# Seven-product matmul groups: weight sums made by accumulating transfers from POOL's queue, products in another order, two raw buffers in place of three

## The chip, the core and the metric

One core of one Trainium2 chip runs the whole program. The metric is the device time in microseconds from one launch to its end. Engines are named PE (TensorE), ACT (ScalarE), DVE (VectorE), POOL (GpSimd) and SP (SyncE, which here only issues transfers).

## What is computed

A sequence of 512 tokens of width 1024 runs through three transformer layers in float32. What matters here are the three feed-forward parts, two with a squared relu and one gated:

```python
def _mlp(x, w_up, w_down):            # layers "mlp0" and "mlp1", hidden width 4096
    h = jax.nn.relu(x @ w_up)
    return (h * h) @ w_down
# the third, "ffn", hidden width 2816: (silu(x @ w_1) * (x @ w_2)) @ w_ffn_out
```

## The kernel before

**Split matmuls.** Every matmul of the projections runs as three fp32r matmuls: each operand is split into a high part (the value rounded to fp32r) and a low part (the rest), and high x high, high x low and low x high are accumulated in PSUM. One matmul of 128x128 by 128x512 is one of the three.

**Chunks.** Weights come in chunks of at most 2048 numbers a partition (1 MB). Chunk `c` uses slot `c % 2` of three pairs of buffers: `RAW` (as loaded), `WH` (high, written by ACT's `split`, L1450) and `WL` (low, written by DVE's `split`, L2115). SP's `load` waits until `lo_ready` says that chunk c-2 is split, and issues the transfer into its raw buffer. ACT's `split` waits for the transfer (`raw_in`) and for `chunk_done` of c-2, so that the `WH` slot is free. DVE's `split` follows half by half and raises `lo_ready`, on which PE waits before it starts the chunk. Both halves are 1024 wide.

**Stages.** mlp0 and mlp1 have four rounds each, ffn three. A round first makes eight feature tiles (up projection, four chunks, each 48 matmuls) and then multiplies them by the matching rows of the down weights. In the first three rounds of an mlp and the first two of ffn, eight in all and called groups 0 to 7 (`SEVEN`), this second step is a 2x2 block product with seven block products instead of eight. The tiles fall into even and odd ones, the tokens and output columns into halves. Each group has four weight blocks, `block(k, n)` with k the parity of the tile and n the half of the columns, 1 MB each. Sums and differences of the activations are made by DVE tile pair by tile pair while the up projection runs (`first_sum`, `other_sums`, in `SQ_T` and `S_T`) and are split by `pair_high` and `pair_low`. Of the seven weight operands three are blocks and four are sums of blocks.

**A group's chunks** are d to d+6, with d = `SEVEN_AT[g]`; d+7 is the next round's first up chunk. A product is 24 matmuls, on two PSUM banks, and DVE's `taken` (L2170 to L2181) adds or copies them into quadrants of `Y` or common parts in `X` (for ffn in other buffers), which frees the banks for the product after the next. `common_sums` puts the parts together in the following round.

**Weight sums before.** SP loads block(0,0) into the raw buffer of d, block(0,1) into that of d+1, and block(1,1) into a third buffer, `THIRD`, in the arena `ar` (L457). DVE forms the four sums with subtractions: `first_weights` (L2157, one instruction of 2048) before the last pair of tiles, and three pairs of 1024 (L2199, L2210, L2222) between the splits of `seven`. It raises `weight_sums` after each, on which ACT waits for its high halves (`high_half`, L1453) and SP before it loads block(1,0) for d+5 and before d+7. DVE's low halves of these chunks are `low_half` (L2123).

**POOL's stream** is in program order: small statistics, bias and mask loads, and in `load_gb` (L3031) two broadcasts of 512 KB into `GB`. In mlp0 and mlp1 `load_gb` stands in wait of `s_("ln0_y")` or `s_("ln2_y")` for T = 4 tiles. DVE's `plus_bias` (L2501) raises these, one tile for each of the four up chunks of the first round, the fourth within the last chunk, after `first_weights` and `sum_of_even`. So the fourth comes just ahead of groups 0 and 3.

Of the kernel before, what the change touches and what calls it, by code (L numbers as in the profile page):

```python
# [18 lines left out]
P = 128  # L19
# [52 lines left out]
UNLOADED = {d + x for d in SEVEN_AT for x in (2, 3, 4, 6)}  # L72


def raw_loads(c):

    return sum(x not in UNLOADED for x in range(c % 2, c + 1, 2))

# [61 lines left out]
def build(nc, a, out):  # L140
# [11 lines left out]
    def sem(name):  # L152
        return ctx.enter_context(nc.semaphore(name))
# [58 lines left out]
    raw_more = [sem(f"raw_more{s}") for s in range(2)]  # L212
    hi_ready, lo_ready = sem("hi_ready"), sem("lo_ready")
# [35 lines left out]
    weight_sums, third_in = sem("weight_sums"), sem("third_in")  # L249
# [16 lines left out]
    def slot(c):  # L266
        return c % 2

# [121 lines left out]
    S_T, THIRD = cut(0, 768), cut(8192, CH)  # L390
# [35 lines left out]
    def _(sp):  # L426
# [23 lines left out]
        def load_seven(g, down, k0):  # L450

            d = SEVEN_AT[g]
            def block(k, n):
                return down.rearrange("(k two p) n -> p k two n", p=P, two=2)[:, k0 // 2:k0 // 2 + 4, k, 512 * n:512 * n + 512]
            load(d, slot(d), (grid(RAW[slot(d)], 4, 512), block(0, 0)))
            load(d + 1, slot(d + 1), (grid(RAW[slot(d + 1)], 4, 512), block(0, 1)))
            sp.dma_start(grid(THIRD, 4, 512), block(1, 1)).then_inc(third_in, 16)  # L457
            sp.wait_ge(weight_sums, 7 * g + 5)
            load(d + 5, slot(d + 5), (grid(RAW[slot(d + 5)], 4, 512), block(1, 0)))
            sp.wait_ge(weight_sums, 7 * g + 7)  # L460
# [127 lines left out]
    def _(pe):  # L588
# [359 lines left out]
        def seven(g, name, i):  # L948

            d, (_, ra, _, n0, _, _) = SEVEN_AT[g], BASE[name]  # L950
            lower, upper, centre = A[0:2], A[2:4], C
            low, high = [slice(256 * m, 256 * m + 256) for m in range(2)]
            even, odd = [lambda v, p, m, k=k: v[:, 2 * p + k, m] for k in range(2)]
            part = lambda x: lambda v, p, m: v[:, p, 256 * x:256 * x + 256]
            last = i == (1 if name == "ffn" else 2)
            for q, (of, m, event, banks) in enumerate((
                    (even, low, 1, lower), (even, high, 1, upper), (part(1), None, 3, centre), (part(2), None, 3, upper),
                    (part(0), None, 3, centre), (odd, low, 2, upper), (odd, high, 2, centre))):
                pe.wait_ge(lo_ready, d + q + 1)
# [476 lines left out]
    def _(act):  # L1436
        def split(c, per=0, i=0, more=None, halves=(0, 1)):
# [4 lines left out]
            act.wait_ge(raw_in[s], 16 * raw_loads(c) + i * (16 * (per // 2)))  # L1442
# [12 lines left out]
        def high_half(c, src, half):  # L1455

            at = slice(1024 * half, 1024 * half + 1024)
            act.wait_ge(chunk_done, c - 1)
            copy(WH[slot(c)][:, at], src[:, at]).then_inc(hi_ready, 1)

# [6 lines left out]
        def seven(g):  # L1467

            d = SEVEN_AT[g]
            first = RAW[slot(d)]  # L1470
            act.wait_ge(weight_sums, 7 * g + 1)
            high_half(d + 1, first, 0)
            pair_high(g, 3, 0)
            high_half(d + 1, first, 1)
            pair_high(g, 3, 1)
            for half in range(2):
                act.wait_ge(weight_sums, 7 * g + 2 + half)
                high_half(d + 2, first, half)
            pair_high(g, 3, 2)
            act.wait_ge(third_in, 16 * g + 16)  # L1480
            for half in range(2):
                high_half(d + 3, THIRD, half)
            for half in range(2):
                act.wait_ge(weight_sums, 7 * g + 4 + half)
                high_half(d + 4, THIRD, half)
            split(d + 5)
            for half in range(2):
                act.wait_ge(weight_sums, 7 * g + 6 + half)
                high_half(d + 6, first, half)
            split(d + 7)  # L1490
# [608 lines left out]
    def _(dve):  # L2099
# [19 lines left out]
        def low_half(c, src, half):  # L2119

            at = slice(1024 * half, 1024 * half + 1024)
            dve.wait_ge(hi_ready, 2 * c + half + 1)
            x = tt(WL[slot(c)][:, at], src[:, at], f32(WH[slot(c)][:, at]), ALU.subtract)  # L2123
            if half:
                x.then_inc(lo_ready, 1)

# [5 lines left out]
        def first_sum(g, p, ready):  # L2132

            dve.wait_ge(*ready)
            tt(SQ_T[:, 0, 256:512], SQ_T[:, 0, 256:512], SQ_T[:, 1, 256:512], ALU.add).then_inc(pair_sums, 1)  # L2135
            dve.wait_ge(pair_sums, pair_event(g, p, 1))

        def other_sums(g, p):
# [3 lines left out]
            tt(S_T[:, 512:768], SQ_T[:, 1, 0:256], S_T[:, 256:512], ALU.subtract).then_inc(pair_sums, 1)  # L2142
# [8 lines left out]

        def first_weights(g):

            d = SEVEN_AT[g]
            dve.wait_ge(raw_in[slot(d + 1)], 16 * raw_loads(d + 1))
            dve.wait_ge(lo_ready, d + 1)
            tt(RAW[slot(d)][:], RAW[slot(d + 1)][:], RAW[slot(d)][:], ALU.subtract).then_inc(weight_sums, 1)  # L2157
# [25 lines left out]
        def seven(g, name, i, biased=None, ready=None):  # L2183

            d = SEVEN_AT[g]
            raw, other, upper, centre = RAW[slot(d)], RAW[slot(d + 1)], A[2:4], C
            halves = [slice(1024 * half, 1024 * half + 1024) for half in range(2)]
# [5 lines left out]
            low_half(d + 1, raw, 0)  # L2193
            pair_low(g, 3, 0)
            low_half(d + 1, raw, 1)
            dve.wait_ge(third_in, 16 * g + 16)
            dve.wait_ge(lo_ready, d + 2)
            for at in halves:
                tt(raw[:, at], THIRD[:, at], raw[:, at], ALU.subtract).then_inc(weight_sums, 1)  # L2199
            low_half(d + 2, raw, 0)  # L2200
            low_half(d + 2, raw, 1)
            other_sums(g, 3)
            pair_low(g, 3, 1)
            pair_low(g, 3, 2)
            taken(g, 1, five, upper, fresh)
            low_half(d + 3, THIRD, 0)
            low_half(d + 3, THIRD, 1)
            dve.wait_ge(lo_ready, d + 4)
            for at in halves:
                tt(THIRD[:, at], THIRD[:, at], other[:, at], ALU.subtract).then_inc(weight_sums, 1)  # L2210
            taken(g, 2, six, centre, fresh)
            low_half(d + 4, THIRD, 0)
            low_half(d + 4, THIRD, 1)
            if biased:
                dve.wait_ge(*biased)
            taken(g, 3, quadrant(0, 1), upper, kept)
            low_half(d + 5, other, 0)
            low_half(d + 5, other, 1)
            dve.wait_ge(raw_in[slot(d + 5)], 16 * raw_loads(d + 5))
            dve.wait_ge(lo_ready, d + 3)  # L2220
            for at in halves:
                tt(raw[:, at], other[:, at], raw[:, at], ALU.subtract).then_inc(weight_sums, 1)  # L2222
            taken(g, 4, sum_seven(name), centre, fresh)
            low_half(d + 6, raw, 0)
            low_half(d + 6, raw, 1)
            taken(g, 5, quadrant(0, 0), upper, kept)
# [3 lines left out]
        def common_sums(name, g, at):  # L2230
# [6 lines left out]
            for x in range(2):  # L2237
# [3 lines left out]
                elif at == 1:  # L2241
                    dve.wait_ge(common_one, 2 * SUMMED.index(name) + 2)
                    then(tt(quadrant(0, 1)[:, x, :], quadrant(0, 1)[:, x, :], six[:, x, :], ALU.add))
                    tt(quadrant(0, 1)[:, x, :], quadrant(0, 1)[:, x, :], five[:, x, :], ALU.add)
                else:
# [3 lines left out]
                    if name == "ffn":  # L2249
                        z = tt(y, y, five[:, x, :], ALU.add)  # L2250
                    else:
                        then(tt(five[:, x, :], five[:, x, :], seventh[:, x, :], ALU.add))
# [250 lines left out]
        def mlp(name, before, ln, n):  # L2503
# [8 lines left out]
            for i in range(3):  # L2512
                g = (0 if name == "mlp0" else 3) + i
                for j in range(4):
                    split(c0 + 11 * i + j + 1)
                    if j == 3:
                        first_weights(g)
# [416 lines left out]
        for n in range(2):  # L2934
            for p in range(4):
                split(c + 2 * p + 1)
                split(c + 2 * p + 2)
                if p == 3:
                    first_weights(6 + n)
# [47 lines left out]
    def _(pool):  # L2987
# [64 lines left out]
        load_gb(a["ln_mlp_g"][0], a["ln_mlp_b"][0])  # L3052
        pool.wait_ge(s_("toeplitz_out"), 16)
# [16 lines left out]
        load_gb(a["ln_mlp_g"][1], a["ln_mlp_b"][1])  # L3070

# [30 lines left out]
        load_gb(a["norm_gains_2"][0, 3])  # L3102

# [18 lines left out]
```

## Time and profile before

| | |
|---|---|
| time, median of 3 runs | 2385.11 us (2384.94 to 2386.81) |
| profiled execution | span 2384.7 us, no time of its own beside it |
| PE | 2361.6 us, 99% |
| weight loads into PE | 1951.9 us, 82% |
| DVE | 1382.1 us, 58% |
| ACT | 963.6 us, 40% |
| POOL | 73.9 us, 3% |
| transfers | 220.25 MB, 92 GB/s on average |

The span is that of the profiled execution from the first to the last instruction. Busy shares are over the whole span. Matmuls overlap, so two that follow each other every 0.23 us are each shown as 0.39 us long; the distance of their starts is what counts.

### The profile page before, as it was taken

How to read it: one execution, taken by the hardware profiler on the slowest of the kernel's cores; microseconds unless marked ns; L12 is line 12 of the kernel's file. 1: busy time of each engine (PE TensorE's matmuls, PEld its weight loads, DVE VectorE, ACT ScalarE, POOL GpSimd, SP SyncE). 2: the span in 40 equal slices, each digit the busy share in tenths (PEclk: the TensorE clock that was granted, in tenths of full speed). 3: DMA queues.
4: the chain of work that ended last, by engine and by line, in shares of the span. 5: the costliest groups of instructions: out<-in, count | busy, mean ns of one | idle time of the engine just before them, and what ended most of it. 6: DMA issues, size and time to landing. Idle time of an engine off the chain costs nothing.

```text
span 2384.7 us, 29276 instructions
## 1 busy us (share of the span) xinstructions
PE 2361.6 (99%) x11460; PEld 1951.9 (82%) x11460; DVE 1382.1 (58%) x2079; ACT 963.6 (40%) x1731; POOL 73.9 (3%) x148
## 2 busy tenths in 40 slices
PE   8999999999999999999999999999999999999998
PEld 8778888888888888888888888888877888888887
DVE  4667877766678787676545223223356535574655
ACT  4434443325545344345444233332245534433323
POOL 3000000000000000000000001000000000000000
PEclk9999999999999999999999999999999999999999
DMA  4124324332212322323222322223321122323232
GB/s 143 54 73 133 124 79 142 106 106 94 66 54 89 124 89 88 124 89 106 85 75 85 109 89 75 84 71 99 100 71 54 54 88 95 100 71 124 88 123 71
DMA packets 177237, 220.25 MB, mean 92 GB/s; under 512 B 10031, under 2 KB 131084, under 8 KB 176864
## 3 DMA queue, kind: packets, MB, share of 16 engines
q1 hardware_dynamic: 173152, 204.82, 26.8%
q0 software_dynamic: 3968, 13.81, 1.8%
q8 instruction: 81, 1.33, 0.2%
q14 instruction: 36, 0.29, 0.0%
HBM read 216.48 MB, written 5.28 MB: 93 GB/s over the span
## 4 chain that ended last, share of the span: by engine, by line
PE 95%; DVE 3%; ACT 1%; issue 0%; DMA 0%; SPq 0%; DVEq 0%
PE B L590 45%; PE A L590 41%; PE C L590 7%; PE C L1052 1%; DVE ar L2324 0%; DVE WL L2115 0%; PE C L1315 0%; DMA X<-in_x 0%; PE C L1161 0%; DVE Y L2446 0%; DVE st L2427 0%; PE C L657 0%; PE C L876 0%; DVE X L2919 0%; PE A L657 0%
## 5 line engine op out<-in xcount | busy, mean ns | idle before, releaser
L2115 DVE TENSOR_TENSOR WL<-RAW,WH 128x1024 fp32r<-128x1024 f32 (+3 forms) x346 | 395.6, 1184 | 383.4 <-ACT WH L1450 383.0
L590 PE MATMUL B<-XH,WH 128*128 128x512 f32 (+1 forms) x1432 | 542.6, 383 | 1.4 <-ACT XH L1507 0.8
L590 PE MATMUL B<-XH,WL 128*128 128x512 f32 (+1 forms) x1432 | 534.9, 377 | 0.0
L590 PE MATMUL B<-XL,WH 128*128 128x512 f32 (+1 forms) x1432 | 520.4, 379 | 2.9 <-DVE XL L2271 2.8
L1450 ACT ACTIVATE WH<-RAW 128x1024 fp32r<-128x1024 f32 (+4 forms) x362 | 353.0, 1025 | 406.7 <-PE A L590 266.2
L590 PEld LDWEIGHTS B<-XH,WH 128*128 128x128 f32 x1432 | 269.2, 188 | 68.4 <-issue 14.1
L590 PEld LDWEIGHTS B<-XH,WL 128*128 128x128 f32 x1432 | 269.2, 188 | 50.4
L590 PEld LDWEIGHTS B<-XL,WH 128*128 128x128 f32 x1432 | 260.4, 189 | 52.4 <-DVE XL L2271 4.6
L590 PE MATMUL A<-WH,XH 128*128 128x512 f32 (+2 forms) x688 | 260.7, 379 | 0.0
L590 PE MATMUL A<-WH,XL 128*128 128x512 f32 (+2 forms) x688 | 259.2, 377 | 0.0
L590 PE MATMUL A<-WL,XH 128*128 128x512 f32 (+2 forms) x688 | 259.1, 377 | 0.0
L590 PE MATMUL A<-WH,YH 128*128 128x512 f32 x608 | 237.6, 391 | 0.2 <-DVE WL L2115 0.2
L590 PE MATMUL A<-WH,YL 128*128 128x512 f32 x608 | 236.8, 390 | 0.0
L590 PE MATMUL A<-WL,YH 128*128 128x512 f32 x608 | 236.7, 389 | 0.0
L590 PEld LDWEIGHTS A<-WH,XH 128*128 128x128 f32 x688 | 129.5, 188 | 23.8 <-issue 1.0
L590 PEld LDWEIGHTS A<-WH,XL 128*128 128x128 f32 x688 | 129.4, 188 | 23.2
L590 PEld LDWEIGHTS A<-WL,XH 128*128 128x128 f32 x688 | 129.6, 188 | 22.9
L590 PEld LDWEIGHTS A<-WH,YH 128*128 128x128 f32 x608 | 114.1, 188 | 24.9 <-DVE WL L2115 0.7
L590 PEld LDWEIGHTS A<-WH,YL 128*128 128x128 f32 x608 | 114.1, 188 | 24.0
L590 PEld LDWEIGHTS A<-WL,YH 128*128 128x128 f32 x608 | 114.2, 188 | 23.0
L590 PE MATMUL A<-ar 64*128 64x256 f32 (+7 forms) x512 | 112.6, 438 | 0.0
L1453 ACT ACTIVATE YH<-ar 128x512 fp32r<-128x512 f32 (+1 forms) x86 | 51.6, 627 | 133.8 <-DVE ar L2135 81.4
(368 smaller groups left out, 2967.9 us busy)
## 6 DMA issues: line engine op xcount, KB each, us to landing
RAW<-in_w_in SPq DMA_DIRECT2D x33, 1024.0 KB, 5.1
RAW<-in_mlp_w_up SPq DMA_DIRECT2D x32, 1024.0 KB, 5.3
RAW<-in_mlp_w_down SPq DMA_DIRECT2D x26, 1024.0 KB, 5.1
RAW<-in_w_in SPq DMA_DIRECT2D x48, 512.0 KB, 4.5
RAW<-in_w_ffn_in SPq DMA_DIRECT2D x22, 1024.0 KB, 5.1
RAW<-in_w_ffn_out SPq DMA_DIRECT2D x8, 1024.0 KB, 5.0
ar<-in_mlp_w_down SPq DMA_DIRECT2D x6, 1024.0 KB, 7.6
RAW<-in_mla_w_o SPq DMA_DIRECT2D x4, 1024.0 KB, 5.0
```

The source lines that it names most:

```text
L590: return nc.tensor.matmul(dst, l, r, start=first, stop=last)
L1052: r = nc.tensor.transpose(C[kb][:, tok(x)], W_S[:, z, h, blk * P:blk * P + P], ident[:])
L1450: nc.scalar.activation(WH[s][:, part], RAW[s][:, part], ACT.Copy).then_inc(hi_ready, 1)
L1453: return nc.scalar.activation(dst, src, ACT.Copy, scale=scale)
L2115: x = tt(WL[s][:, part], RAW[s][:, part], f32(WH[s][:, part]), ALU.subtract)
```

## The change

- SP loads only three blocks of a group as chunks: block(0,0) into d, block(1,0) into d+1, block(1,1) into d+3 (`SEVEN_PLAIN`).
- POOL issues four transfers that add a block from HBM onto what the raw buffer holds (`add_seven`, `SEVEN_ADDED`): block(0,1) for d+2, block(1,1) for d+4, block(0,1) for d+5, block(1,0) for d+6. Each waits for `lo_ready` of chunk c-2 and raises `raw_added` of its slot.
- `first_weights` and the three pairs of DVE subtractions are gone, with `THIRD`, `high_half`, `low_half`, `weight_sums` and `third_in`. ACT and DVE use the ordinary `split` for all seven chunks.
- The order of the products, their activation operands, the places that `taken` writes and signs in the activation sums and in `common_sums` change to fit.
- In POOL's stream the transfers of groups 0 to 2 stand behind the `load_gb` that waits for `ln0_y`, those of groups 3 to 5 behind that for `ln2_y`, those of 6 and 7 at the end.

```diff
+SEVEN_PLAIN, SEVEN_ADDED = {0: (0, 0), 1: (1, 0), 3: (1, 1)}, {2: (0, 1), 4: (1, 1), 5: (0, 1), 6: (1, 0)}
+ADDED_AT = {d + q for d in SEVEN_AT for q in SEVEN_ADDED}
...
         def load_seven(g, down, k0):
...
-            load(d, slot(d), (grid(RAW[slot(d)], 4, 512), block(0, 0)))
-            load(d + 1, slot(d + 1), (grid(RAW[slot(d + 1)], 4, 512), block(0, 1)))
-            sp.dma_start(grid(THIRD, 4, 512), block(1, 1)).then_inc(third_in, 16)
-            sp.wait_ge(weight_sums, 7 * g + 5)
-            load(d + 5, slot(d + 5), (grid(RAW[slot(d + 5)], 4, 512), block(1, 0)))
-            sp.wait_ge(weight_sums, 7 * g + 7)
+            for q, (k, n) in SEVEN_PLAIN.items():
+                c = SEVEN_AT[g] + q
+                load(c, slot(c), (grid(RAW[slot(c)], 4, 512), seven_block(down, k0, k, n)))
...
             for q, (of, m, event, banks) in enumerate((
-                    (even, low, 1, lower), (even, high, 1, upper), (part(1), None, 3, centre), (part(2), None, 3, upper),
-                    (part(0), None, 3, centre), (odd, low, 2, upper), (odd, high, 2, centre))):
+                    (even, low, 1, lower), (odd, low, 2, upper), (even, high, 1, centre), (part(2), None, 3, upper),
+                    (part(1), None, 3, centre), (part(0), None, 3, upper), (odd, high, 2, centre))):
...
-            act.wait_ge(raw_in[s], 16 * raw_loads(c) + i * (16 * (per // 2)))
+            act.wait_ge((raw_added if c in ADDED_AT else raw_in)[s], 16 * raw_loads(c) + i * (16 * (per // 2)))
...
-            tt(SQ_T[:, 0, 256:512], SQ_T[:, 0, 256:512], SQ_T[:, 1, 256:512], ALU.add).then_inc(pair_sums, 1)
+            tt(SQ_T[:, 0, 256:512], SQ_T[:, 0, 256:512], SQ_T[:, 1, 256:512], ALU.subtract).then_inc(pair_sums, 1)
...
             first_sum(g, 3, ready)
-            low_half(d + 1, raw, 0)
+            split(d + 1, halves=(0,))
             pair_low(g, 3, 0)
-            low_half(d + 1, raw, 1)
-            dve.wait_ge(third_in, 16 * g + 16)
-            dve.wait_ge(lo_ready, d + 2)
-            for at in halves:
-                tt(raw[:, at], THIRD[:, at], raw[:, at], ALU.subtract).then_inc(weight_sums, 1)
-            low_half(d + 2, raw, 0)
-            low_half(d + 2, raw, 1)
+            split(d + 1, halves=(1,))
             other_sums(g, 3)
             pair_low(g, 3, 1)
+            split(d + 2)
             pair_low(g, 3, 2)
...
+            taken(g, 1, quadrant(0, 0), upper, kept)
+            split(d + 3)
+            taken(g, 2, five, centre, fresh)
+            split(d + 4)
             taken(g, 3, quadrant(0, 1), upper, kept)
...
+            split(d + 5)
+            taken(g, 4, six, centre, fresh)
+            split(d + 6)
+            taken(g, 5, sum_seven(name), upper, fresh)
             split(d + 7)
             taken(g, 6, quadrant(1, 0), centre, kept)
...
                     split(c0 + 11 * i + j + 1)
-                    if j == 3:
-                        first_weights(g)
                     sum_of_even(squared(i, j, 0))
...
         pool.wait_ge(s_("ln0_y"), T)
         load_gb(a["ln_mlp_g"][0], a["ln_mlp_b"][0])
+        def add_seven(g, down, k0):
+            for q, (k, n) in SEVEN_ADDED.items():
+                c = SEVEN_AT[g] + q
+                pool.wait_ge(lo_ready, c - 1)
+                pool.dma_start(grid(RAW[slot(c)], 4, 512), seven_block(down, k0, k, n), accum_op=ALU.add).then_inc(raw_added[slot(c)], 16)
+        for i in range(3):
+            add_seven(i, a["mlp_w_down"][0], 8 * i)
         pool.wait_ge(s_("toeplitz_out"), 16)
```

## Rows read from the trace of the kernel before

**Rows 1.** The page, part 1: busy us, share, instructions of each engine.

```profile
PE 2361.6 (99%) x11460; PEld 1951.9 (82%) x11460; DVE 1382.1 (58%) x2079; ACT 963.6 (40%) x1731; POOL 73.9 (3%) x148
```

**Rows 2.** Waits of PE: releaser, us in total, times, longest.

```profile
PE B L590 <- DVE WL L2115: 0.3, 1, 0.3
```

**Rows 3.** Chain in order of time, 772 to 812: start us, us, what.

```profile
772.73 10.89 PE A L590 x48
...
794.61 5.62 PE C L590 x24
...
805.69 5.75 PE C L590 x24
```

**Rows 4.** The same chain, 2241 to 2281.

```profile
2241.92 10.88 PE A L590 x48
...
2258.29 5.49 PE A L590 x24
...
2274.72 5.44 PE C L590 x24
```

**Rows 5.** Timeline of PE, ACT, POOL and SP: start us, us, engine, line, operation.

```profile
772.57 0.39 PE L590 MATMUL A<-WH,YH 128*128 128x512 f32 x1
...
796.42 2.01 ACT L1450 ACTIVATE WH<-RAW 128x1024 fp32r<-128x1024 f32 x2 [4.39 <-DMA RAW<-in_mlp_w_down]
...
773.83 0.56 POOL L3031 DMA_DIRECT2D GB<-in_ln_mlp_g  x1 [143.94 <-DVE Y L2501]
774.38 0.55 POOL L3031 DMA_DIRECT2D GB<-in_ln_mlp_b  x1
...
242.31 0.37 SPq L438 DMA_DIRECT2D RAW<-in_mlp_w_down  x1
242.72 0.84 SPq L457 DMA_DIRECT2D ar<-in_mlp_w_down  x1
```

**Rows 6.** DVE groups by form: busy us, mean ns, idle before.

```profile
L2199 DVE TENSOR_TENSOR RAW<-ar,RAW 128x1024 f32<-128x1024 f32 x16 | 18.9, 1222 | 0.8
...
L2157 DVE TENSOR_TENSOR RAW<-RAW 128x2048 f32<-128x2048 f32 x8 | 18.3, 2292 | 0.8
```

**Rows 7.** Timeline of DVE around group 3.

```profile
766.59 2.35 DVE L2115 TENSOR_TENSOR WL<-RAW,WH 128x1024 fp32r<-128x1024 f32 x2
...
772.31 1.22 DVE L2501 TENSOR_TENSOR Y<-Y,GB 128x1024 f32<-128x1024 f32 x1
...
776.37 1.22 DVE L2123 TENSOR_TENSOR WL<-RAW,WH 128x1024 fp32r<-128x1024 f32 x1
...
782.32 0.42 DVE L2140 TENSOR_TENSOR ar<-ar 128x256 f32<-128x256 f32 x1
...
783.12 0.69 DVE L2150 TENSOR_TENSOR YL<-ar,YH 128x512 fp32r<-128x512 f32 x1
...
784.99 1.28 DVE L2178 COPY X<-A 128x512 f32<-128x512 f32 x2
...
797.52 2.36 DVE L2123 TENSOR_TENSOR WL<-RAW,WH 128x1024 fp32r<-128x1024 f32 x2 [1.51 <-ACT WH L1450]
...
803.27 2.35 DVE L2123 TENSOR_TENSOR WL<-RAW,WH 128x1024 fp32r<-128x1024 f32 x2
```

**Rows 8.** Issues of transfers: line, operation, count, KB each, median us to landing.

```profile
RAW<-in_mlp_w_down SPq DMA_DIRECT2D x26, 1024.0 KB, 5.1
...
ar<-in_mlp_w_down SPq DMA_DIRECT2D x6, 1024.0 KB, 7.6
...
toeplitz<-heads POOLq DMA_DIRECT2D x1, 3072.0 KB, 15.4
...
GB<-in_ln_mlp_b POOLq DMA_DIRECT2D x2, 512.0 KB, 5.0
```

**Rows 9.** Two stretches: us, busy (instructions) of PE, PEld, DVE, ACT, POOL, granted clock, DMA share, GB/s.

```profile
772.00:811.00 39.00, 39.00 (x171) 31.55 (x170) 34.88 (x39) 16.80 (x18) 1.10 (x2) 1.00 0.34 108
...
2241.00:2280.00 39.00, 39.00 (x174) 32.15 (x173) 33.43 (x37) 16.37 (x17) 0.00 (x0) 1.00 0.25 82
```

More of the change, by code:

```diff
@@ L71 @@
 SEVEN_AT = [BASE[name][0] + at for name, _, at in SEVEN]
-UNLOADED = {d + x for d in SEVEN_AT for x in (2, 3, 4, 6)}
+SEVEN_PLAIN, SEVEN_ADDED = {0: (0, 0), 1: (1, 0), 3: (1, 1)}, {2: (0, 1), 4: (1, 1), 5: (0, 1), 6: (1, 0)}
+ADDED_AT = {d + q for d in SEVEN_AT for q in SEVEN_ADDED}
 def raw_loads(c):
-    return sum(x not in UNLOADED for x in range(c % 2, c + 1, 2))
+    return sum((x in ADDED_AT) == (c in ADDED_AT) for x in range(c % 2, c + 1, 2))
 def constants():
@@ L212, in build @@
     raw_more = [sem(f"raw_more{s}") for s in range(2)]
+    raw_added = [sem(f"raw_added{s}") for s in range(2)]
     hi_ready, lo_ready = sem("hi_ready"), sem("lo_ready")
@@ L248, in build @@
     pair_sums, sums_hi, sums_lo = sem("pair_sums"), sem("sums_hi"), sem("sums_lo")
-    weight_sums, third_in = sem("weight_sums"), sem("third_in")
     seven_free = [sem(f"seven_free{x}") for x in range(2)]
@@ L267, in slot, with seven_block @@
         return c % 2
+    def seven_block(w, k0, k, n):
+        return w.rearrange("(k two p) n -> p k two n", p=P, two=2)[:, k0 // 2:k0 // 2 + 4, k, 512 * n:512 * n + 512]
     def unit_number(i, u):
@@ L389, in build @@
     R_T, SQ_T = cut(0, 2, S), cut(1024, 2, S)
-    S_T, THIRD = cut(0, 768), cut(8192, CH)
+    S_T = cut(0, 768)
     W_V, W_Q, W_KG = cut(0, T, 256), cut(1024, 2, 2, S), cut(3072, SWA_KV, S)
@@ L450, in load_seven @@
         def load_seven(g, down, k0):
-            d = SEVEN_AT[g]
-            def block(k, n):
-                return down.rearrange("(k two p) n -> p k two n", p=P, two=2)[:, k0 // 2:k0 // 2 + 4, k, 512 * n:512 * n + 512]
-            load(d, slot(d), (grid(RAW[slot(d)], 4, 512), block(0, 0)))
-            load(d + 1, slot(d + 1), (grid(RAW[slot(d + 1)], 4, 512), block(0, 1)))
-            sp.dma_start(grid(THIRD, 4, 512), block(1, 1)).then_inc(third_in, 16)
-            sp.wait_ge(weight_sums, 7 * g + 5)
-            load(d + 5, slot(d + 5), (grid(RAW[slot(d + 5)], 4, 512), block(1, 0)))
-            sp.wait_ge(weight_sums, 7 * g + 7)
+            for q, (k, n) in SEVEN_PLAIN.items():
+                c = SEVEN_AT[g] + q
+                load(c, slot(c), (grid(RAW[slot(c)], 4, 512), seven_block(down, k0, k, n)))
         def load_mlp(name, up, down):
@@ L1453, in copy @@
             return nc.scalar.activation(dst, src, ACT.Copy, scale=scale)
[L1455 to L1459, printed above, removed]
         def pair_high(g, p, x):
@@ L1469, in seven @@
             d = SEVEN_AT[g]
-            first = RAW[slot(d)]
-            act.wait_ge(weight_sums, 7 * g + 1)
-            high_half(d + 1, first, 0)
+            split(d + 1, halves=(0,))
             pair_high(g, 3, 0)
-            high_half(d + 1, first, 1)
+            split(d + 1, halves=(1,))
             pair_high(g, 3, 1)
-            for half in range(2):
-                act.wait_ge(weight_sums, 7 * g + 2 + half)
-                high_half(d + 2, first, half)
+            split(d + 2)
             pair_high(g, 3, 2)
[L1480 to L1490, printed above, removed]
+            for q in range(3, 8):
+                split(d + q)
         def hi_transposed(name, dst, ks=range(8)):
@@ L2117, in split @@
                     x.then_inc(lo_ready, 1)
[L2119 to L2125, printed above, removed]
         def sum_of_even(ready):
@@ L2141, in other_sums @@
             dve.wait_ge(pair_sums, pair_event(g, p, 2))
-            tt(S_T[:, 512:768], SQ_T[:, 1, 0:256], S_T[:, 256:512], ALU.subtract).then_inc(pair_sums, 1)
+            tt(S_T[:, 512:768], SQ_T[:, 1, 0:256], S_T[:, 256:512], ALU.add).then_inc(pair_sums, 1)
         def pair_low(g, p, x):
@@ L2150, in pair_low @@
             tt(dst, of, f32(hi), ALU.subtract).then_inc(sums_lo, 1)
[L2152 to L2157, printed above, removed]
         def common_parts(name):
@@ L2185, in seven @@
             d = SEVEN_AT[g]
-            raw, other, upper, centre = RAW[slot(d)], RAW[slot(d + 1)], A[2:4], C
-            halves = [slice(1024 * half, 1024 * half + 1024) for half in range(2)]
+            upper, centre = A[2:4], C
             five, six = common_parts(name)
@@ L2192, in seven @@
             first_sum(g, 3, ready)
-            low_half(d + 1, raw, 0)
+            split(d + 1, halves=(0,))
             pair_low(g, 3, 0)
-            low_half(d + 1, raw, 1)
-            dve.wait_ge(third_in, 16 * g + 16)
-            dve.wait_ge(lo_ready, d + 2)
-            for at in halves:
-                tt(raw[:, at], THIRD[:, at], raw[:, at], ALU.subtract).then_inc(weight_sums, 1)
-            low_half(d + 2, raw, 0)
-            low_half(d + 2, raw, 1)
+            split(d + 1, halves=(1,))
             other_sums(g, 3)
             pair_low(g, 3, 1)
+            split(d + 2)
             pair_low(g, 3, 2)
[L2205 to L2213, printed above, removed]
             if biased:
                 dve.wait_ge(*biased)
+            taken(g, 1, quadrant(0, 0), upper, kept)
+            split(d + 3)
+            taken(g, 2, five, centre, fresh)
+            split(d + 4)
             taken(g, 3, quadrant(0, 1), upper, kept)
[L2217 to L2226, printed above, removed]
+            split(d + 5)
+            taken(g, 4, six, centre, fresh)
+            split(d + 6)
+            taken(g, 5, sum_seven(name), upper, fresh)
             split(d + 7)
@@ L2242, in common_sums @@
                     dve.wait_ge(common_one, 2 * SUMMED.index(name) + 2)
-                    then(tt(quadrant(0, 1)[:, x, :], quadrant(0, 1)[:, x, :], six[:, x, :], ALU.add))
+                    then(tt(quadrant(0, 1)[:, x, :], quadrant(0, 1)[:, x, :], six[:, x, :], ALU.subtract))
                     tt(quadrant(0, 1)[:, x, :], quadrant(0, 1)[:, x, :], five[:, x, :], ALU.add)
@@ L2249, in common_sums @@
                     if name == "ffn":
-                        z = tt(y, y, five[:, x, :], ALU.add)
+                        z = tt(y, five[:, x, :], y, ALU.subtract)
                     else:
-                        then(tt(five[:, x, :], five[:, x, :], seventh[:, x, :], ALU.add))
+                        then(tt(five[:, x, :], five[:, x, :], seventh[:, x, :], ALU.subtract))
                         z = stt(y, y, ALPHA, five[:, x, :], ALU.mult, ALU.add)
@@ L2937, in _ @@
                 split(c + 2 * p + 2)
-                if p == 3:
-                    first_weights(6 + n)
                 sum_of_even(product(p, 0))
@@ L3070, in _ @@
         load_gb(a["ln_mlp_g"][1], a["ln_mlp_b"][1])
+        for i in range(3):
+            add_seven(3 + i, a["mlp_w_down"][1], 8 * i)
         def heads_rms(name):
@@ L3102, in _ @@
         load_gb(a["norm_gains_2"][0, 3])
+        for i in range(2):
+            add_seven(6 + i, a["w_ffn_out_2"][0], 8 * i)
     ctx.close()
```

## Prediction

> **What bounds the kernel now.** I read the page first: TensorE is busy 99% of the span and VectorE 58% [rows 1]. So VectorE time counts only where TensorE stands behind it. The second view, TensorE's waits, asks where that is: the largest entry for a weight split is 0.3 us in the whole program [rows 2]. The third view is the chain inside the seven-product groups. Group 3 (the first of mlp1) runs from 772.73 to 811.45, 38.7 us. Its first two products take 10.89, the fifth 5.62 and the last 5.75 [rows 3]. Group 7 shows the floor, 5.44 to 5.49 each [rows 4]. Seven times 5.44 is 38.1 us. The worst group is thus 0.6 us above the floor, and all eight cannot give back more than 8 x 0.6 = 4.8 us, 0.2% of the kernel. Group 7 taken eight times (2274.72 + 5.44 - 2241.92 = 38.24) gives 1.2 us. I take 1.5 us as the gain if all goes well, with 0 and 4.8 as bounds.
>
> I call the start of product 0 of group 3 (its first matmul, 772.57) t = 0 [rows 5]. Products then start near 0, 5.45, 10.9, 16.4, 21.9, 27.4 and 32.9.
>
> **What is removed.** Per group VectorE loses one 128x2048 subtraction of 2.29 us and six of 128x1024 at 1.22 (three lines of x16 that cost the same; one is shown), together 9.6 us, 77 us in eight groups [rows 6]. On TensorE's path that is worth only the 0 to 4.8 us above: what hides the subtractions is the running product. ACT loses nothing but waits for them. The relu-side sums keep their number; only signs, the order and one event change. Product 1 now takes the odd tiles and so needs the second sum: VectorE is through the low half of chunk d+1 at 777.59 (t+5.0), two sums of 0.42 and a subtraction of 0.69, with the gaps between them, make t+6.65 [rows 7], and product 1 asks for that tile at 5.45 + 3 x 1.36 = t+9.5. No cost.
>
> **What is added: 32 accumulating transfers of 1 MB from POOL's queue, each in a loop of its own.** Four chunks of a group (d+2, d+4, d+5, d+6) come by adding a block from HBM onto the raw buffer that chunk c-2 has left. The loop is: low half of c-2 done, POOL issues, L us until the sum has landed, ACT's high half, VectorE's low half, product c. Its fixed parts have rows. From the end of the VectorE instruction at 773.53 to POOL's issue at 773.83 is 0.3 [rows 5, 7]. From ACT's start on a landed chunk (796.42) to the end of VectorE's two halves on the same chunk is 3.46 (797.52 + 2.36 - 796.42) [rows 5, 7]. From VectorE's last low half (803.27 + 2.35 = 805.62) to the product that waits for it (805.69) is nothing [rows 3, 7]. So chunk c must have landed by its product's start less 3.5:
>
> - d+2 by 7.4, d+4 by 18.4, d+5 by 23.9, d+6 by 29.4.
>
> **The unknown, L.** No accumulating transfer is in this trace. The nearest rows: a plain 1 MB load lands in 5.1 us; the third block, issued 0.41 behind such a load (242.31 and 242.72), lands in 7.6, so two megabytes take 8.0; I divide that into 2.6 of latency and 2 x 2.7 of data, which makes a single one 5.3, near the 5.1; 3 MB from HBM to HBM take 15.4 [rows 5, 8]. An accumulation has to read its destination as well as its source. If that read costs as much as the first, data takes 5.4 and L = 2.6 + 5.4 = 8.0. Below, L is no less than the plain 5.1. Above, if read, read and write follow each other, 15.4 is the nearest row. I take 8.0, since the second read goes through the same sixteen engines and the pair of loads shows them filled already by plain ones. Two accumulations in a row come out 5.4 apart. The time of an issue on POOL, 0.54 for a plain one [rows 5], is within L.
>
> **An ordinary group (six of eight).** The low half of d is done at 766.59 + 2.35 = 768.94, t-3.6 [rows 7]. So d+2 is issued at t-3.3 and lands at 4.7, in time for 7.4. Its high half starts when product 0 has ended (5.5), and VectorE, free at 6.65, is through at t+9.1. d+4 is issued at 9.4 and lands at 17.4 (limit 18.4). The low half of d+3 follows the evacuation of product 1 (1.28) and ends near 15.0; d+5 is issued at 15.2 and lands at 23.2 (limit 23.9). The low half of d+4 ends at 17.4 + 3.5 = 20.9; d+6 is issued at 21.2 and lands at 29.2 (limit 29.4). So at L = 8.0 all four fit, the last by 0.2: cost nothing, with no reserve. The DMA engines, busy 0.25 of a group's time without broadcasts [rows 9], would carry four accumulations of 5.4 and three plain loads of 2.7, about 30 of 38.7 us.
>
> **Groups 0 and 3 are different.** There POOL's stream first waits for the last tile of Y plus bias and then issues two broadcasts into GB, before any accumulation. Without the 2.29 us subtraction ahead of it, that VectorE instruction ends at 773.53 - 2.29 = 771.24 and POOL issues at 771.54, t-1.0. The two issues take 1.1 [rows 5], so the first accumulation leaves at t+0.1 and not at t-3.3. The second broadcast landed 5.5 us after the first one's issue (774.38 + 5.0 - 773.83), so t+4.5 [rows 5, 8]. The accumulation's data comes behind it: 4.5 + 5.4 = 9.9, against 7.4. TensorE stands 2.5 us before product 2. Queued behind the waiting ACT instruction is the high half of the last sums, behind VectorE's the evacuation of product 1. They only matter from product 3 on. The late chain goes on: low half at 13.4, d+4 issued 13.7, landed 21.7 against 18.4 + 2.5, another 0.8. Low half 25.2, d+6 issued 25.5, landed 33.5 against 29.4 + 3.3, another 0.8. In all 4.1 us for each of the two groups.
>
> **Sum at L = 8.0:** 2 x 4.1 = 8.2, less 1.5, is +6.7 us. SP's queue loses its two waits for subtractions and issues d+3 and d+7 earlier; d+7, after the low half of d+5 (26.7), is needed at 38.3 - 3.5, 8 us for a load of 5.1, no cost. On POOL the bias loads and later broadcasts stand behind the last accumulation of their layer, and each waits for a product or a tile that comes after it anyway. TensorE's granted clock is 1.00, the 2.4 GHz level, in both stages shown [rows 9], and the stalls are a few us with the engine busy between them; I cost the clock at nothing. The rows are of an execution whose span is 2384.7; the three timed runs lie at 2384.9 to 2386.8, so I set the sum on the median, 2385.1: 2391.8, say 2392.
>
> **How the sum goes with L.** The same working gives (ordinary group, groups 0 and 3, total after the 1.5): L = 7.5 about 0, 2.6, +4; L = 9: data 6.4, d+6 late by 1.5 and d+5 by 0.3, so 1.8 and 7.1, +24; L = 10: 4.8 and 11.1, +50; L = 15.4: 21 and 33, +190. It is flat under 7.5 and steep above 9: three of the four accumulations then queue on each other.
>
> **Rivals.** A is the forecast: L from 7.5 to 9.5, +4 to +37 us, most of it in groups 0 and 3 at first. Chance 0.42.
>
> B, the transfers are hidden: L under 7.5, because the second read overlaps the first (about half of a plain load is latency by the working above). Then groups 0 and 3 cost at most 2.6 each, the rest nothing, and the gain takes some back: 2383 to 2389. For it speaks that the DMA engines are busy only 0.25 to 0.34 of a group's time [rows 9]; against it what a second megabyte cost. Chance 0.35. The Trainium skill has a rule that ends here: "DMA: Bandwidth & Descriptors", section "Anatomy of one DMA", gives 2.0 us plus bytes by 436 GB/s. By it, as an estimate, a plain megabyte is 4.4 and one read twice 6.8, and the kernel would be unchanged. The trace's plain load, 5.1, is above that rule. The same skill's "Collectives: The Full Stack", section "The bandwidth ceiling", says that a reducing transfer is slowed by its two source reads and not by the addition, a measured ratio of 1.93; no run here shows it yet.
>
> C, the accumulation itself is slow: L above 9.5, the adding unit or the read of the destination before each write becoming the pace. Then d+4, d+5 and d+6 each hold TensorE in every group: 2422 to 2440 at L up to 10, up to 2575 by the 15.4 us row. For it speaks only that nothing here excludes it. Chance 0.18.
>
> D, on the other side: faster by over 0.2%. The one mechanism is that TensorE's slow pitch inside groups (5.6 against 5.44) is all caused by VectorE's lateness, in every group as in group 3, and L stays under 7. It decides only if the full 4.8 us come back, giving 2380. Group 7, whose VectorE does the same subtractions and which runs at 5.44 to 5.49, speaks against it. Chance 0.05.
>
> **Numbers.** A timed comparison of this kernel tells about 0.2% (4.8 us) from nothing. Of A, 0.35 lies above that and 0.07 within. With C's 0.18 slower has 0.53; same has B's 0.35 and the 0.07, 0.42; faster 0.05. The range goes from 2383 (B with its gain) to 2435 (L = 10) and leaves out D's 0.05 and the larger part of C. A alone is 2389 to 2422.
>
> **What the changed profile would show.** The issues of the accumulations with their time to landing: 8 us right, 5 to 7 is B, above 9.5 is C. ACT's waits for those transfers instead of for VectorE's subtractions. TensorE gaps before products 2, 4 and 6 of groups 0 and 3, and almost none in groups 6 and 7. POOL's first accumulation of group 3 about a microsecond after its second GB issue. DMA share in a group near 0.8. VectorE's busy time lower by 77 us. The prediction is wrong if L is far from 8, if the GB broadcasts do not delay the first accumulation, or if TensorE's pitch itself changes under the heavier traffic into SBUF, which I cost at nothing because group 7's fourth product, with the load of d+5 beside it, takes 5.49 and the seventh 5.44 [rows 4].

## The result and the profile after

The changed kernel takes 2408.9 us (2408.3 to 2409.4, 4 runs) against 2385.1 (2384.9 to 2386.8), ratio 1.0097 [1.0082, 1.0111]: 23.8 us slower. The forecast was slower, at 2392, with a range of 2383 to 2435: the way and the range hold, but the sum had 6.7 us, less than a third of what came.

The page first: where [rows 1] had TensorE at 99% of a span of 2384.7, it has 98% of 2407.6. In the chain that ended last, TensorE falls from 95% to 84%, transfers rise from nothing to 6% of the span and VectorE from 3% to 6% (the chain line of the kernel before is shown first). VectorE is busy 73 us less.

```profile
PE 95%; DVE 3%; ACT 1%; issue 0%; DMA 0%; SPq 0%; DVEq 0%
```

```profile
span 2407.6 us, 29190 instructions
...
PE 2367.1 (98%) x11460; PEld 1952.7 (81%) x11460; DVE 1309.4 (54%) x2023; ACT 960.4 (40%) x1731; POOL 115.2 (5%) x180
...
q0 software_dynamic: 20864, 47.37, 10.1%
...
PE 84%; DMA 6%; DVE 6%; ACT 2%; issue 1%; POOL 0%; SPq 0%; DVEq 0%; ACTq 0%; POOLq 0%
```

The issues of the accumulations (queue POOLq), columns as in [rows 8]. This is the unknown L of the prediction, the time from issue to landing: 8.6 to 8.7 us where it was taken as 8.0.

```profile
RAW<-in_mlp_w_down POOLq DMA_DIRECT2D x24, 1024.0 KB, 8.7
...
RAW<-in_w_ffn_out POOLq DMA_DIRECT2D x8, 1024.0 KB, 8.6
```

TensorE's waits. [rows 2] had at most 0.3 us for a weight split; now 17.2 us stand there, ahead of products of the groups, which run on the banks A and C.

```profile
PE C L590 <- DVE WL L2096: 15.6, 11, 4.7
...
PE A L590 <- DVE WL L2096: 1.6, 3, 1.0
```

The chain of group 3, which [rows 3] show as TensorE alone. Not one of the first six products is in it now: from POOL's broadcasts on it runs through three accumulations. Each is followed by ACT's and VectorE's split of the landed chunk, and the first two splits by 0.28 to 0.29 us to POOL's next issue.

```profile
781.70 1.10 POOL GB L2976 x2
...
782.82 12.25 DMA RAW<-in_mlp_w_down
...
795.09 1.06 ACT WH L1450
...
796.17 2.37 DVE WL L2096 x2
798.55 0.29 issue
798.84 8.77 DMA RAW<-in_mlp_w_down
...
811.38 8.36 DMA RAW<-in_mlp_w_down
...
823.27 5.73 PE C L590 x24
```

In group 1, one of the ordinary ones, the loop d+2, d+4, d+6 only takes over after product 0, and its transfers take 8.4:

```profile
346.75 5.50 PE A L590 x24
...
356.07 8.38 DMA RAW<-in_mlp_w_down
...
368.23 8.43 DMA RAW<-in_mlp_w_down
...
380.19 5.73 PE C L590 x24
```

One thing is new that the prediction had put at nothing. TensorE stood 4.7 us before product 2 of group 3, and the next matmuls follow each other in 0.43 us and no longer in 0.23:

```profile
798.59 0.80 PE L590 MATMUL C<-WH,YH 128*128 128x512 f32 x1 [4.66 <-DVE WL L2096]
799.18 0.63 PE L590 MATMUL C<-WL,YH 128*128 128x512 f32 x1
799.61 0.63 PE L590 MATMUL C<-WH,YL 128*128 128x512 f32 x1
```

The stretches ahead of it, just after it and later (columns as in [rows 9]) show the granted clock at 1.00, then at 0.52, nearly all of it at the 1.2 GHz level, then at 1.00 again:

```profile
783.00:793.50 10.50, 10.50 (x47) 8.65 (x47) 5.44 (x8) 3.65 (x5) 1.15 (x1) 1.00 1.05 226
...
798.50:801.80 3.30, 3.21 (x8) 2.59 (x9) 3.30 (x6) 1.22 (x2) 1.29 (x1) 0.52 0.27 33
802.00:806.00 4.00, 4.00 (x19) 3.31 (x18) 1.07 (x2) 0.00 (x0) 1.27 (x1) 1.00 1.09 193
```

The time of each group, from the first matmul of product 0 to the first of what follows product 6, in us, worked out from the timelines of TensorE (first starts; the last column is the sum).

| kernel | g0 | g1 | g2 | g3 | g4 | g5 | g6 | g7 | sum |
|---|---|---|---|---|---|---|---|---|---|
| before | 38.4 | 38.4 | 38.4 | 38.7 | 38.6 | 38.6 | 38.3 | 38.2 | 307.5 |
| changed | 46.1 | 39.2 | 39.9 | 46.0 | 39.5 | 40.4 | 39.6 | 39.7 | 330.3 |
| e1, first accumulation ahead | 39.1 | 39.0 | 39.2 | 39.5 | 39.3 | 39.1 | 39.0 | 39.2 | 313.3 |
| e7, between the tiles and the broadcasts | 41.7 | 39.3 | 39.1 | 41.6 | 39.2 | 40.2 | 39.4 | 39.4 | 319.8 |
| e2, plain transfers | 38.3 | 38.2 | 38.2 | 38.6 | 38.2 | 38.2 | 38.2 | 38.2 | 306.3 |
| e3, halves | 44.7 | 38.3 | 38.2 | 43.0 | 38.3 | 38.3 | 38.2 | 38.2 | 317.3 |
| e4, e1 and e3 | 38.3 | 38.2 | 38.2 | 38.3 | 38.3 | 38.2 | 38.2 | 38.2 | 306.1 |
| e5, long rows | 44.3 | 38.3 | 38.6 | 44.7 | 38.3 | 38.3 | 38.2 | 38.6 | 319.2 |
| e6, two accumulations | 45.3 | 38.6 | 39.1 | 44.9 | 38.2 | 38.3 | 38.2 | 38.2 | 321.0 |

The eight groups explain nearly the whole: 330.3 - 307.5 = 22.8, and the spans differ by 22.9 (the medians of the timed runs by 23.8). Groups 0 and 3 hold 15.0 of it (7.7 and 7.3), the six others 7.8 (0.8 to 1.8 each).

### The profile page after: what moved, and what is told of

The parts are those of the page before. It is cut to its first block, busy times and chain, and to the rows that moved or that the text cites. A ratio compares the mean times of both kernels' runs of the same rounds, so it can differ in the third digit from the quotient of the medians.

```text
span 2407.6 us, 29190 instructions
## 1 busy us (share of the span) xinstructions
PE 2367.1 (98%) x11460; PEld 1952.7 (81%) x11460; DVE 1309.4 (54%) x2023; ACT 960.4 (40%) x1731; POOL 115.2 (5%) x180
## 4 chain that ended last, share of the span: by engine, by line
PE 84%; DMA 6%; DVE 6%; ACT 2%; issue 1%; POOL 0%; SPq 0%; DVEq 0%; ACTq 0%; POOLq 0%
PE B L590 43%; PE A L590 35%; DMA RAW<-in_mlp_w_down 5%; PE C L590 3%; DVE WL L2096 3%; DMA RAW<-in_w_ffn_out 1%; ACT WH L1450 1%; PE C L1052 1%; DVE ar L2273 0%; PE C L1315 0%; DMA X<-in_x 0%; PE C L1161 0%; DVE Y L2395 0%; DVE st L2376 0%; DVE XL L2220 0%
## 5 line engine op out<-in xcount | busy, mean ns | idle before, releaser
L2096 DVE TENSOR_TENSOR WL<-RAW,WH 128x1024 fp32r<-128x1024 f32 (+4 forms) x442 | 509.3, 1192 | 439.8 <-ACT WH L1450 439.0
L1450 ACT ACTIVATE WH<-RAW 128x1024 fp32r<-128x1024 f32 (+4 forms) x442 | 434.0, 1030 | 538.1 <-PE A L590 295.2
L590 PE MATMUL A<-WH,YH 128*128 128x512 f32 x544 | 212.7, 391 | 0.2 <-DVE WL L2096 0.2
L590 PE MATMUL A<-WH,YL 128*128 128x512 f32 x544 | 211.9, 390 | 0.0
L590 PE MATMUL A<-WL,YH 128*128 128x512 f32 x544 | 211.8, 389 | 0.0
L590 PEld LDWEIGHTS A<-WL,XH 128*128 128x128 f32 x688 | 129.4, 188 | 22.9
L590 PEld LDWEIGHTS A<-WH,YH 128*128 128x128 f32 x544 | 102.1, 188 | 22.3 <-DVE WL L2096 0.7
L590 PEld LDWEIGHTS A<-WH,YL 128*128 128x128 f32 x544 | 102.1, 188 | 21.3
L590 PEld LDWEIGHTS A<-WL,YH 128*128 128x128 f32 x544 | 102.1, 188 | 20.7
```

The source lines that it names most:

```text
L590: return nc.tensor.matmul(dst, l, r, start=first, stop=last)
L1450: nc.scalar.activation(WH[s][:, part], RAW[s][:, part], ACT.Copy).then_inc(hi_ready, 1)
L2096: x = tt(WL[s][:, part], RAW[s][:, part], f32(WH[s][:, part]), ALU.subtract)
```

## The experiments

**e1: the first accumulation of groups 0 and 3 ahead.** The rest of POOL's stream is as it was; the third layer needs no such edit.

```diff
+        add_seven(0, a["mlp_w_down"][0], 0, (2,))
         pool.wait_ge(s_("ln0_y"), T)
         load_gb(a["ln_mlp_g"][0], a["ln_mlp_b"][0])
...
+            add_seven(i, a["mlp_w_down"][0], 8 * i, SEVEN_ADDED if i else (4, 5, 6))
```

> Only the first accumulation of groups 0 and 3 changes place: POOL issues it ahead of the wait for the biased tiles and of the two GB broadcasts. My theory (the accumulation's own 8.4 to 8.7 us in every group, plus the broadcasts ahead of the first one in groups 0 and 3): the first accumulation of group 3 leaves 3.3 us before product 0 and lands in time, the gap of 4.8 us before product 2 and the slow matmuls after it go, groups 0 and 3 take 39.2 to 40.4 us like the others instead of 46.0, so 12 to 13 us less than the changed kernel: 2396. Rival (the broadcasts don't matter, the late start of a layer's first group does, or the memory is slower there): groups 0 and 3 stay above 44, 2405 or more.

Measured: 2394.1 us (2391.1 to 2395.4), ratio to before 1.0034 [1.0021, 1.0048]. Groups 0 and 3 take 39.1 and 39.5; the other six lie at 39.0 to 39.3, so some of them came down too. The profiled execution is the fastest of the five, 3.0 us under their median. POOL's timeline at group 0 shows the first accumulation leaving ahead of the broadcasts, 3.3 us before product 0:

```profile
253.45 1.32 POOL L3002 DMA_DIRECT2D RAW<-in_mlp_w_down  x1 [27.51 <-DVE WL L2096]
255.64 0.56 POOL L2976 DMA_DIRECT2D GB<-in_ln_mlp_g  x1 [0.86 <-DVE Y L2450]
```

What remains is one wait in each group, before product 6:

```profile
PE C L590 <- DVE WL L2096: 4.4, 8, 0.9
```

So the place of that accumulation behind the tiles and the broadcasts cost about 15 us by the medians (13.5 in groups 0 and 3 of the two profiles), the slow clock with it. The rival that a layer's first group is slow whatever stands ahead of this transfer falls. Whether the wait for the tiles or the broadcasts weigh more, this run doesn't say; e7 does.

**e7: between.** The same accumulation behind the wait for the tiles, ahead of the two broadcasts.

```diff
         pool.wait_ge(s_("ln0_y"), T)
+        add_seven(0, a["mlp_w_down"][0], 0, (2,))
         load_gb(a["ln_mlp_g"][0], a["ln_mlp_b"][0])
...
```

> As in e1 the first accumulation of groups 0 and 3 stands ahead of the two GB broadcasts, but behind the wait for the biased tiles, so it leaves 1.0 us before product 0 and not 3.3. In the changed kernel that chunk lands 11.7 us after product 0's start, 7.4 would do. If most of the excess is the broadcasts' data and issues ahead of it, the chunk lands at -1.0 + 8.4 to 9 = 7.4 to 8.0, the stall before product 2 is 0 to 0.6 us, TensorE's clock stays up, and the whole is 2393 to 2397. Rival (the late start behind the tiles is the larger part, and broadcasts issued just after it share the engines and hold it as long): landing at 10 or later, stalls of 2.5 us or more in both groups, 2401 or more.

Measured: 2397.8 us (2396.6 to 2398.8), ratio 1.0047 [1.0033, 1.0061], 0.8 us above what I expected. The chain of group 0 shows why:

```profile
255.55 8.24 DMA RAW<-in_mlp_w_down
...
267.57 9.58 DMA RAW<-in_mlp_w_down
...
280.92 8.36 DMA RAW<-in_mlp_w_down
```

The first one lands at 263.79, t+7.1 (product 0 starts at 256.69), and product 2 doesn't wait. But its successor leaves 1.4 us later than in an ordinary group and takes 9.6 us. The broadcasts had landed by then (8.6 and 10.2 us after the start of product 0, the successor leaves at 10.9); what it meets are the plain load of d+3, which lands at 12.6, and the next accumulation, issued at 16.4. What makes the 9.6 was not tried. TensorE then stands 2.0 us before product 4. The order of the broadcasts is thus most of the loss (46 to 41.7 us for a group), and the start 2.2 us later than in e1 goes with the rest (41.7 to 39.1). I had worked out only the first of the three transfers.

**e2: plain transfers.** This kernel leaves the additions out, so four of seven products use a block instead of a sum.

```diff
-                pool.dma_start(grid(RAW[slot(c)], 4, 512), seven_block(down, k0, k, n), accum_op=ALU.add).then_inc(raw_added[slot(c)], 16)
+                pool.dma_start(grid(RAW[slot(c)], 4, 512), seven_block(down, k0, k, n)).then_inc(raw_added[slot(c)], 16)
```

> The four transfers of a group stay on POOL's queue at the same places and with the same waits, but overwrite the raw buffer and add nothing, so the weights of four products are a block and not a sum. My theory (reading the destination is what costs): time to landing 5.1 to 5.5 us, six groups at 38.1 to 38.4, groups 0 and 3 at most 1 us above, and as VectorE's subtractions are gone too the whole is 2382 to 2386. Rival 1 (software descriptors are the cost, POOL needs 1.28 us for one such issue): landing stays above 7.5 and the time above 2395. Rival 2 (the new order of the products or their sums costs by itself): landing 5, but groups above 38.6 and 2388 or more.

Measured: 2385.5 us (2384.0 to 2386.4, 11 runs), ratio 0.9998 [0.9989, 1.0007]. The issues and the queue:

```profile
q0 software_dynamic: 12672, 47.37, 6.1%
...
RAW<-in_mlp_w_down POOLq DMA_DIRECT2D x24, 1024.0 KB, 5.7
...
RAW<-in_w_ffn_out POOLq DMA_DIRECT2D x8, 1024.0 KB, 5.4
```

Three things follow. First, the queue, its waits and the traffic of blocks cost nothing; the addition does. Taking the 1.8% that this queue had before from its share, 32 plain transfers keep the sixteen engines busy for 4.3% of 2382.5 us, 3.2 us each, and 32 accumulations for 8.3% of 2407.6, 6.2 us each, 1.95 times as much. The Trainium skill ("Collectives: The Full Stack", section "The bandwidth ceiling") has a reducing transfer between cores slowed by its second source read, 1.93 times. The trace's 1.95 agrees with that ratio; that it is the read and not the adding which costs, no run here separates. Second, the new order of products costs nothing. Third, the groups together are 1.2 us shorter than before (1.4 in e4 below). That is all that the removed VectorE work was worth on TensorE's path.

**e3: halves.** Each accumulation is two of 512 KB with semaphores of their own, issued and split half by half. POOL's wait for `toeplitz_out` moves ahead of the one for `ln0_y`, since that semaphore serves again.

```diff
+                pool.wait_ge(lo_first, halves_before(c - 2) + 2)
+                pool.dma_start(dst[:, 0:2, :], src[:, 0:2, :], accum_op=ALU.add).then_inc(raw_first[slot(c)], 16)
                 pool.wait_ge(lo_ready, c - 1)
-                pool.dma_start(grid(RAW[slot(c)], 4, 512), seven_block(down, k0, k, n), accum_op=ALU.add).then_inc(raw_added[slot(c)], 16)
+                pool.dma_start(dst[:, 2:4, :], src[:, 2:4, :], accum_op=ALU.add).then_inc(raw_added[slot(c)], 16)
...
             for half in halves:
+                if added and half:
+                    act.wait_ge(raw_added[s], 16 * raw_loads(c))
```

> Each accumulation is issued as two of 512 KB, each as soon as VectorE is through with that half of the old chunk, and ScalarE starts on each half when it has landed. My theory (the loop of landing 8.4, splitting 3.5 and 0.3 to POOL, 12.2 us against two products of 10.9): the loop becomes about 10 us, the waits before products 4 and 6 go in the six ordinary groups (8 us in all), and groups 0 and 3 get 1 to 2.5 us shorter each: 2395 to 2399. Rival (the DMA engines are full in a group, 0.75 to 0.87 busy, so more and smaller transfers are no faster): ordinary groups stay at 39.2 to 40.4 and the time at 2406 to 2411.

Measured: 2395.5 us (2392.0 to 2397.3), ratio 1.0038 [1.0024, 1.0052]. The six ordinary groups are at 38.2 to 38.3, groups 0 and 3 at 44.7 and 43.0. The DMA engines are about as full as before the edit (busy 0.85 of group 1, against 0.87 in the changed kernel), and still the waits are gone. The rival that full DMA engines are the limit falls: what held the products was the length of one loop. TensorE's remaining waits in the groups are two, before product 2 of groups 0 and 3:

```profile
PE C L597 <- DVE WL L2106: 6.6, 2, 3.5
```

After the one of group 0 (the last matmul before it starts at 267.86, the next at 271.76) the clock falls again. The 0.62 of the stretch that follows is a mean over both levels, 0.50 at first and 1.00 at its end:

```profile
260.00:268.00 8.00, 8.00 (x37) 6.45 (x35) 4.66 (x7) 2.33 (x3) 0.00 (x0) 1.00 1.07 220
272.00:279.00 7.00, 7.00 (x20) 5.54 (x21) 4.04 (x5) 1.08 (x2) 3.62 (x3) 0.62 1.01 161
```

**e4: both edits.**

> Both edits together, the first accumulation of groups 0 and 3 ahead of the broadcasts and every accumulation in two halves. My theory: all eight groups at 38.1 to 38.5, so the time of before or up to 3 us less, 2382 to 2386. Rival (full DMA engines): the gain of the first edit alone, 2394 to 2398.

Measured: 2384.4 us (2384.1 to 2386.1, 11 runs) beside 2385.9 of the kernel before, ratio 0.9995 [0.9986, 1.0004]. The chain of group 3, as in [rows 3], is TensorE alone and has every product at 5.44 to 5.49:

```profile
772.38 10.93 PE A L597 x48
783.32 5.44 PE C L597 x24
...
794.25 5.49 PE C L597 x24
...
805.24 5.44 PE C L597 x24
```

This kernel leaves none of the work out, with the accumulations in place. It can't be told from the kernel before by its time; the groups' sum is 1.4 us lower, and the profiled spans (2383.1 and 2384.7) differ by 1.6.

**e5: long rows.** The accumulations read rows of 8 KB for each partition from other places of the same tensor, so other weights are added.

```diff
-                pool.dma_start(grid(RAW[slot(c)], 4, 512), seven_block(down, k0, k, n), accum_op=ALU.add).then_inc(raw_added[slot(c)], 16)
+                pool.dma_start(RAW[slot(c)][:], down.rearrange("(b p two) n -> b p (two n)", p=P, two=2)[k0 // 2 + 2 * k + n], accum_op=ALU.add).then_inc(raw_added[slot(c)], 16)
```

> The four accumulations take the same megabyte of each block's size from HBM as rows of 8 KB for each partition instead of four of 2 KB (so other weights are added, the products are those of other numbers). In the changed kernel a plain transfer on this queue is 272 packets and an accumulation 528, and the DMA engines are busy 6.2 us with one against 3.2. My theory (the destination is read as well, so bytes are what costs): landing stays at 8.0 to 8.7 and the time at 2402 to 2410. Rival (packets of 2 KB are what costs, half of that could be saved with long rows): packets fall to about 272, landing to 6 or less, six groups at 38.2 to 38.4 and about 2396 to 2399, with groups 0 and 3 still late.

Measured: 2397.9 us (2397.4 to 2398.6), ratio 1.0049 [1.0035, 1.0063]. The time is outside what I expected and inside the rival's. The landing is at the lower edge of what I expected (8.0 to 8.7) and far from the rival's 6:

```profile
q0 software_dynamic: 8576, 47.37, 9.4%
...
RAW<-in_mlp_w_down POOLq DMA_DIRECT2D x24, 1024.0 KB, 8.0
...
RAW<-in_w_ffn_out POOLq DMA_DIRECT2D x8, 1024.0 KB, 7.9
```

An accumulation went from 528 packets to 144 ((8576 - 3968) / 32), a fourth, and the engines are still busy 7.6% of 2395.6 us, 5.7 us each, instead of 6.2. So the number of packets is little of the price. The landing came 0.4 to 0.7 us sooner. POOL's issue, which lies within it, is 0.4 shorter (0.86 in place of 1.27). That was enough: ordinary groups fell from 39.2-40.4 to 38.2-38.6. That is the edge that the working put near L = 8; I had not used it for this expectation.

Group 0 of this run also shows that a wait of this size does not always bring the clock down. TensorE stood 3.2 us before product 2, and the granted clock stayed at 1.00; product 2 took 5.6 us. In group 3 of the same execution it stood 3.5 us, and product 2 took 8.1.

```profile
271.58 0.50 PE L590 MATMUL C<-WH,YH 128*128 128x512 f32 x1 [3.24 <-DVE WL L2096]
```

```profile
271.60:275.00 3.40, 3.40 (x15) 2.79 (x16) 3.40 (x5) 1.11 (x2) 0.87 (x1) 1.00 0.56 70
```

**e6: two accumulations.** d+4 and d+6 are plain transfers, so two products use a block instead of a sum.

```diff
+                op = dict(accum_op=ALU.add) if q in (2, 5) else {}
+                pool.dma_start(grid(RAW[slot(c)], 4, 512), seven_block(down, k0, k, n), **op).then_inc(raw_added[slot(c)], 16)
```

> Only d+2 and d+5 are accumulations, d+4 and d+6 are plain transfers on the same queue (two products use a block in place of a sum). My theory: the loop of one slot (landing, 3.5 of splitting, 0.3) is what holds products 4 and 6, so the six ordinary groups are at 38.2 to 38.4, while groups 0 and 3 keep their first stall, 4 to 5 us with 1 to 2 us of slow matmuls after it: 44 to 45 each, in all 2395 to 2399. Rival (full DMA engines in the group): with half of the accumulations gone half of the 8 us of the ordinary groups stays.

Measured: 2398.9 us (2395.6 to 2399.9), ratio 1.0048 [1.0034, 1.0062]. Groups 4 to 7 are at 38.2 to 38.3, groups 1 and 2 at 38.6 and 39.1, with 0.2 and 0.7 us before product 5; the theory expected none there. So two of six are outside the 38.2 to 38.4 expected, while the time is inside. The six ordinary groups of the changed kernel lie 8.7 us above 38.24 each, those of this one 1.3 us: less than the half that the rival would leave. Groups 0 and 3 keep their first stall. The chain and the stretch behind it in group 0:

```profile
255.62 1.05 POOL GB L2976 x2
256.67 11.97 DMA RAW<-in_mlp_w_down
...
272.16 8.14 PE C L590 x24
```

```profile
272.50:276.00 3.50, 3.50 (x9) 2.73 (x9) 3.50 (x5) 0.79 (x1) 0.69 (x1) 0.50 0.60 156
```

Product 2 takes 8.1 us in this chain, with the granted clock at 0.50, the 1.2 GHz level, in the stretch shown.

## Why the prediction was right, and what was mis-sized

**Bound and gain.** Right. Eight groups could give back 4.8 us at most and 1.5 was taken. With nothing in the way (e2, e4) they give 1.2 to 1.4. VectorE lost 73 us (77 forecast), and no time came of it that the timed runs could tell from nothing.

**The loop.** Right in every fixed part: 0.28 to 0.29 us to POOL's issue, 3.45 from ACT's start to VectorE's end. In group 1 POOL issues at 343.25, 356.07, 361.57 and 368.23, that is at -3.3, 9.5, 15.0 and 21.7 from product 0; the working had -3.3, 9.4, 15.2 and 21.2.

**The sum fell short.** It said +6.7 and +23.8 came, 17 us more. The range is wide and holds it; the size was not forecast well. Of the 17 us, 7.8 are in the ordinary groups, 3.3 are slow clock, 3.5 are what else groups 0 and 3 lost beyond the forecast, 1.5 are the gain that the sum took off and the losses hid, and about 1 lies outside the groups.

**L, the term that was mis-sized.** Taken as 8.0, measured as 8.4 for the three accumulations of group 1's loop and 8.6 to 8.7 as the median. The doubling was right in kind: an accumulation takes 3.0 us longer to land than a plain transfer of e2 (8.7 and 5.7), where I took 2.7, and the plain transfer itself takes 5.7 on this queue and not 5.3. Within the 3.0 is POOL's issue, 1.27 instead of 0.75 for a plain transfer of the same shape. Since the fit at L = 8.0 had 0.2 us of reserve, this put 1.3 us on each ordinary group, 7.8 in all, where the sum had 0. The waits I looked for in groups 0 and 3 alone came in groups 6 and 7 too, before product 6. The working's own line for L = 9 (1.8 each, 7.1 in groups 0 and 3, +24 in total) comes close to the 1.3, 7.5 and +23.8 measured, but partly by luck: L was not 9. The same working at 8.7 gives, as an estimate, 1.2, 6.2 and +18, and what is missing there is mostly the slow clock.

**Groups 0 and 3.** Right in place and cause: e1 takes the excess away, e7 shows the broadcasts as its larger part. Forecast 4.1 us each, measured 7.7 and 7.3. Landing of the first accumulation was set at t+9.9 and came at t+12.2 in group 3. The second broadcast landed in 6.0 us and not 5.0, at t+5.5, and the accumulation 6.8 us behind it and not 5.4. The working had left out one transfer: SP's plain load of d+3 leaves at t+5.0 and so runs beside the late accumulation. It took 9.1 us there, against 5.3 in group 1, where the accumulation has landed by then. How much each cost the other was not tried. The following delays are of the forecast's kind, 0.5 and 1.1 us before products 4 and 6 of group 0.

**The clock.** Wrong. I put it at nothing, since the stalls would be a few us. The first one was 4.1 and 4.7 us and not 2.5, and product 2 took 7.0 to 7.2 us instead of 5.45 in both groups: 3.3 us in all. After the 2.0 us of e7 and the 3.2 of e5's group 0 the clock stayed up, so at the forecast's own 2.5 us this term may have been nothing; that was not tried.

**The rivals.** B (hidden, L under 7.5) would have been right only without the addition: e2. The rule of the Trainium skill that the prediction cited for it ("DMA: Bandwidth & Descriptors", section "Anatomy of one DMA"), 2.0 us and the bytes by 436 GB/s, gives 6.8 for two megabytes, as an estimate; the trace has 8.4. C (slow addition) did not come: the median L is 8.6 to 8.7. Single ones are longer, outside groups 0 and 3 too: 10.7 for the accumulation of d+5 in group 5, the slowest of the ordinary groups (40.4). D (faster) is out by e4, which has nothing of the cost and gains 1.4 us in its groups.

**What is left open.** Why e1, which changes nothing in groups 1, 2 and 4 to 7, has them 0.1 to 1.3 us shorter than the changed kernel. The landings of its transfers are 8.3 to 8.4 in the median and not 8.6 to 8.7. The six groups differ by 3.4 us together, and the profiled execution of e1 lies 3.0 us under the median of its runs, so much of it may be the scatter of that execution; this is not shown. Whether the waits before product 5 in e6 come from other transfers beside the accumulation, which takes 9.0 and 9.5 us there, was not tried. And no run separates the second read from the adding.

## What to carry to other kernels

Before moving work to a transfer, write down the loop it closes, here landing, split and issue against two products, and compare it with the period; the work removed counts only if its engine was what TensorE waited for. A transfer that reads its destination too costs about twice the engine time of a plain one, and when such a loop is just too long, cutting the transfer and its consumer into halves shortens it without moving a byte less. In a queue that waits in program order, look at what stands ahead of the first critical transfer: here two broadcasts that could land later at no cost (e4) took more time, 8.8 us by e7's groups 0 and 3, than the six ordinary groups together, 7.8.

## What the runs showed of the hardware that was not expected

- Twice as many packets, too: on this queue a plain 1 MB in 2 KB rows is 272 packets ((12672 - 3968) / 32), the accumulation 528. With 8 KB rows the accumulation is 144 and lands only 0.4 to 0.7 us earlier.
- POOL's issue of an accumulation takes 1.27 us, of a plain transfer of the same shape 0.75, of an accumulation with 8 KB rows 0.86.
- After waits of 3.0 to 4.9 us in otherwise unbroken matmuls, seven of them in four kernels, the granted clock fell to 0.50 for some 3 to 7 us and then was 1.00 again. One wait of this size, 3.2 us in group 0 of e5, left it at 1.00. After the 2.0 us of e7 the next product took 5.6 us, no longer than others there.
